# Attention scores of two layers: one fp32 product over padded heads, or three fp32r products over half of TensorE's rows, two heads at a time

## What is computed

```
x = rmsnorm(h);  dq, dk, dv, dg, fq, fk, fv, ff, fg = split(x @ w_in[l])
dq, dk = rope(dq), rope(dk)                      # 4 heads of two halves of 64
do = softmax(q1 k1') v - lam * softmax(q2 k2') v # "diff": mask by chunks of 64
fo = softmax(fq fk' + c_i - c_j) v               # "fox": 8 heads of 64, causal,
                                                 # c = cumsum(log_sigmoid(ff + bias))
h = h + concat(norm(do) * silu(dg), fo * silu(fg)) @ w_out[l]
```

## Time and profile before

| | |
|---|---|
| median of three runs | 1998.08 us |
| the profiled execution | 1999.93 us, of which the span from first to last instruction 1998.1 us |
| mean granted clock of TensorE | 0.989 |
| attention of layer 0, "diff" / "fox" | 228.2 to 287.2 / 287.2 to 362 us |
| attention of layer 1, "diff" / "fox" | 616 to 661.9 / 661.9 to 734 us |

### The profile page before, as it was taken

The page is one execution under the profiler, slowest core; times in us unless marked ns, Lnnn a source line. Parts: engine busy times, 40 slices in busy tenths (PEclk is TensorE's granted clock), DMA queues, the critical chain, the costliest instruction groups (busy, mean ns, idle before and its releaser), DMA issues.

```text
span 1998.1 us, 26646 instructions
## 1 busy us (share of the span) xinstructions
PE 1924.0 (96%) x10942; PEld 1643.1 (82%) x10942; DVE 755.9 (38%) x1288; ACT 707.1 (35%) x1328; POOL 712.7 (36%) x342
## 2 busy tenths in 40 slices
PE   7999989999998999999999999899999989999999
PEld 7999878989987887888888877789767768888887
DVE  6422373454125526441112255546676441111001
ACT  3112355321125545223222223335564542222211
POOL 4333201253332114555554423320003325555443
PEclk9999899999999999999999999899999989999999
DMA  4222200122221002233322233210003212222323
GB/s 142 84 76 84 64 1 1 53 85 85 75 79 48 1 11 89 96 95 95 95 90 93 94 111 117 65 43 1 1 1 112 79 53 94 92 93 93 99 87 108
DMA packets 40585, 144.22 MB, mean 72 GB/s; under 512 B 4624, under 2 KB 4880, under 8 KB 40336
## 3 DMA queue, kind: packets, MB, share of 16 engines
q1 hardware_dynamic: 40464, 142.51, 22.2%
HBM read 140.40 MB, written 2.10 MB: 71 GB/s over the span
## 4 chain that ended last, share of the span: by engine, by line
PE 86%; DVE 7%; ACT 3%; issue 1%; DMA 1%; POOL 1%; SPq 0%; DVEq 0%; ACTq 0%
PE ps L353 22%; PE ps L354 22%; PE ps L355 22%; PE ps L820 5%; PE ps L801 5%; PE ps L810 3%; DMA raw<-wstream 1%; PE ps L1965 1%; PE ps L1948 1%; PE ps L937 1%; PE ps L480 1%; POOL wl L349 1%; ACT wh L341 1%; PE ps L1937 1%; DVE xl L409 1%
## 5 line engine op out<-in xcount | busy, mean ns | idle before, releaser
L349 POOL TENSOR_TENSOR wl<-raw,wh 128x1024 fp32r<-128x1024 f32 (+2 forms) x254 | 604.5, 2380 | 863.7 <-ACT wh L341 863.7
L353 PE MATMUL ps<-xh,wh 128*128 128x512 f32 (+1 forms) x1728 | 622.4, 360 | 26.2 <-POOL wl L349 13.6
L354 PE MATMUL ps<-xl,wh 128*128 128x512 f32 (+1 forms) x1728 | 615.7, 356 | 0.0
L341 ACT ACTIVATE wh<-raw 128x1024 fp32r<-128x1024 f32 (+2 forms) x254 | 266.0, 1047 | 983.9 <-PE ps L355 914.0
L355 PE MATMUL ps<-xh,wl 128*128 128x512 f32 (+1 forms) x1728 | 613.9, 355 | 0.0
L353 PEld LDWEIGHTS ps<-xh,wh 128*128 128x128 f32 x1728 | 327.4, 189 | 82.4 <-issue 20.5
L354 PEld LDWEIGHTS ps<-xl,wh 128*128 128x128 f32 x1728 | 327.7, 190 | 49.8 <-issue 1.9
L355 PEld LDWEIGHTS ps<-xh,wl 128*128 128x128 f32 x1728 | 327.8, 190 | 48.3
L1064 POOL TENSOR_TENSOR xl<-xb,xh 128x512 fp32r<-128x512 f32 (+1 forms) x22 | 26.1, 1185 | 329.2 <-ACT xh L973 329.2
L354 PE MATMUL ps<-aL,wh 128*128 128x512 f32 x352 | 139.3, 396 | 0.0
L355 PE MATMUL ps<-aH,wl 128*128 128x512 f32 x352 | 139.1, 395 | 0.0
(11 more groups left out here) (331 smaller groups left out, 2551.1 us busy)
## 6 DMA issues: line engine op xcount, KB each, us to landing
raw<-wstream SPq DMA_DIRECT2D x236, 512.0 KB, 3.5
raw<-wstream SPq DMA_DIRECT2D x16, 384.0 KB, 3.0
raw<-wstream SPq DMA_DIRECT2D x10, 528.0 KB, 3.5
h<-xT SPq DMA_DIRECT2D x4, 528.0 KB, 6.0
out<-h SPq DMA_DIRECT2D x8, 256.0 KB, 3.4
hm<-memT SPq DMA_DIRECT2D x1, 1024.0 KB, 4.8
cst<-const SPq DMA_DIRECT2D x1, 720.5 KB, 8.9
cst<-const SPq DMA_DIRECT2D x1, 320.0 KB, 4.0
```

Source lines behind the costliest of these rows:

```text
L341: e.activation(wh[p % 2][:, 0:n], raw[c % 2][:, 0:n], ACT.Copy).then_inc(*w_hi(p))
L349: e.tensor_tensor(wl[p % 2][:, 0:n], raw[c % 2][:, 0:n], wh[p % 2][:, 0:n].bitcast(F32), ALU.subtract).then_inc(*w_lo(p))
L353: e.matmul(o, w_h, x_h, start=start, stop=False)
L354: e.matmul(o, w_h, x_l, start=False, stop=False)
```

## The change

Queries and keys of a layer are kept unpadded, two heads to a tile (128 partitions, four tiles), as an fp32r part ("hi") and the rest ("lo"). ACT makes the hi part and POOL the lo part (`whole_hi`, `whole_lo`), two tiles at every second projection tile, behind the weight splits; DVE waits for them (`halved`) before it writes `scratch` or `tmpn` again. The clearing of QA, QB goes. A unit's scores are three fp32r products over the 64 partitions of its head; units m and m + 1, in the two halves of the rows, begin together with their terms interleaved, in different PSUM banks. The forget bias rows stand twice, so that each half of the rows has them. For wide units `begin` comes after the value products (`late`). The meta scores become three products each with 128 columns of weights, even heads first, and odd heads after a wait for the even ones, since all share one bank. Buffers move; `Plan` and `Unit` carry them.

```diff
-                e.tensor_tensor(KA[:, c, :], u, v, ALU.add).then_inc(*roped(*key, "add", 1))
-                for j in range(2):
-                    e.tensor_tensor(QA[64 * j:64 * j + 64, 2 * c + j, c0:c0 + n], ...
+            e.tensor_tensor(u, u, v, ALU.add).then_inc(*roped(*key, "add"))
...
+        def halved(on, key):
+            on.wait_ge(*x_hi[("qk",) + key])
+            on.wait_ge(*x_lo[("qk",) + key])
+        def whole_hi(e, on, key):
+            src, done, dh, _ = whole(key)
+            on.wait_ge(*done)
+            e.activation(dh, src, ACT.Copy).then_inc(*x_hi("qk", *key))
+        def whole_lo(e, on, key):
+            src, _, dh, dl = whole(key)
+            on.wait_ge(*x_hi[("qk",) + key])
+            e.tensor_tensor(dl, src, dh.bitcast(F32), ALU.subtract).then_inc(*x_lo("qk", *key))
...
-            e.tensor_tensor(NCh[32:40, :], ncm, NCh[0:8, :].bitcast(F32), ALU.subtract).then_inc(*v_one("ncl", l))
+            for a in (32, 96):
+                e.tensor_tensor(NCh[a:a + 8, :], ncm, NCh[0:8, :].bitcast(F32), ALU.subtract)
+            e.tensor_copy(NCh[64:72, :], NCh[0:8, :]).then_inc(*v_one("ncl", l))
...
-                for q, Q in enumerate(Q_of[l]):
-                    e.memset(Q[:, :, :], 0.0).then_inc(*p_one("clear", l, q))
-            for q in range(PART["dq", l, 0], PART["gate", l, 7] + 1):
+            p = PART["dq", l, 0]
+            for q in range(p, PART["gate", l, 7] + 1):
                 split_lo(e, on, q + 2)
+                for key in ready_at(q - p, l) if q - p < 15 else ready_at(15, l) if q - p == 16 else ():
+                    whole_lo(e, on, key)
...
+                begun = plan.begin.get(s, [])
+                if begun and units[begun[0]].rows:
+                    a, b = begun
+                    pa, pb = scores(a), scores(b)
+                    for ta, tb in zip(units[a].terms, units[b].terms):
+                        ra = part(pa, units[a], ta)
+                        rb = part(pb, units[b], tb)
+                    ra.then_inc(*score(name, a))
+                    rb.then_inc(*score(name, b))
+                    return
...
-                begin(s)
+                late = any(units[u].banks[1] == 2 for u in plan.begin.get(s, []))
+                if not late:
+                    begin(s)
                 for u in plan.flips.get(s - 1, []):
...
+                if late:
+                    begin(s)
...
-                for m in range(8):
-                    o = ps[0:16, 16 * m:16 * m + 16]
-                    r = e.matmul(o, Q[:, m, 0:16], K[:, m // 2, 0:16], start=True, stop=kind == "diff")
+                for m in (0, 2, 4, 6, 1, 3, 5, 7):
+                    q, o = slice(64 * (m % 2), 64 * (m % 2) + 64), ps[:, 16 * m:16 * m + 16]
+                    if m == 1:
+                        on.wait_ge(*one_mm["meta", kind, l, "even"])
+                    for x, y in ((Qh, Kh), (Qh, Kl), (Ql, Kh)):
+                        r = e.matmul(o, x[q, m // 2, 0:128], y[q, m // 2, 0:16], start=x is Qh and y is Kh, ...
...
-                            terms.append((Q[:, m, c0:c0 + 128], K[:, m // 2, a:b], a, b, True, False))
+                            q = slice(64 * (m % 2), 64 * (m % 2) + 64)
+                            for x, y in ((Qh, Kh), (Qh, Kl), (Ql, Kh)):
+                                terms.append((x[q, m // 2, c0:c0 + 128], y[q, m // 2, a:b], a, b, ...
-                                terms.append((pickR[:, m:m + 1].to_broadcast([128, 128]), NCh[:, a:b], ...
+                                terms.append((pickR[q, m:m + 1].to_broadcast([64, 128]), NCh[q, a:b], ...
...
-                            cols=..., ahead=1 if wide else 2 if beside_meta else 3,
+                            cols=..., ahead=(1 if wide else 2) + m % 2, rows=True, P=..., PT=...,
```

More of the change, by code:

```diff
@@ L182, in program, with flipped @@
         d_x = [sem(f"d_x{i}") for i in range(4)]
+        def flipped(name, at):
+            sb("before" + name, [128, 4, L], at=at)
+            P = sb("Pb" + name, [128, 4, L], at=at)
+            sb("between" + name, [128, 4, L], at=at)
+            return P, [sb(f"PT{name}{i}", [128, 640], at=at) for i in range(2)]
         h = sb("h", [128, KT, L])
         swap = ExitStack()
-        QA1, QB1 = (sb(n, [128, 8, L], at=swap) for n in ("QA1", "QB1"))
+        QhB1, QhA1, QlB1, QlA1 = (sb(n, [128, 4, L], F32R, at=swap) for n in ("QhB1", "QhA1", "QlB1", "QlA1"))
+        swap.close()
+        Pb0, PT0 = flipped("0", swap)
         swap.close()
@@ L294, in program @@
         rT, rTneg, rTm = small[:, 192:200], small[:, 200:208], small[:, 208:210]
-        X, Q_of = {0: (xh, xl), 1: (xh1, xl1)}, {0: (QA, QB), 1: (QA1, QB1)}
+        X = {0: (xh, xl), 1: (xh1, xl1)}
+        QK = {("dq", 0): (QhA, QlA), ("fq", 0): (QhB, QlB), ("dq", 1): (QhA1, QlA1), ("fq", 1): (QhB1, QlB1)}
+        for l in range(2):
+            QK["dk", l], QK["fk", l] = (KhA, KlA), (KhB, KlB)
+        P_of = {(0, "diff"): (Pb0, PT0), (0, "fox"): (Pb1, PT1), (1, "diff"): (Pb1, PT1), (1, "fox"): (Pb0, PT0)}
         freed = [[] for _ in range(8)]
@@ L585, in proj_act @@
                 split_hi(e, on, p + j + 2)
+                for key in ready_at(j, l) if j < 15 else ():
+                    whole_hi(e, on, key)
                 if l == 0 and j == 10:
@@ L595, in proj_act @@
                 split_hi(e, on, PART[v, l, 0] + 2)
+                for key in ready_at(15, l) if v == "va0" else ():
+                    whole_hi(e, on, key)
                 for i in (1, 3):
@@ L778, in slot_read @@
             def slot_read(self, u):
-                was = u - 4 * len(self.sets)
+                was = u - 4 * len(self.units[u].P)
                 if was < 0:
@@ L792, in attention_pe, with scores, part @@
             units, name = plan.units, plan.name
-            def begin(s):
-                for u in plan.begin.get(s, []):
-                    x = units[u]
-                    ps = claim(on, *x.banks, prob[name, u])
-                    for s_, done in x.ready:
-                        on.wait_ge(*s_[done])
-                    for lhsT, rhs, lo, hi, start, stop in x.terms:
-                        r = e.matmul(ps[:, x.o0 + lo:x.o0 + hi], lhsT, rhs, start=start, stop=stop)
+            def scores(u):
+                x = units[u]
+                ps = claim(on, *x.banks, prob[name, u])
+                for s_, done in x.ready:
+                    on.wait_ge(*s_[done])
+                return ps
+            def part(ps, x, term):
+                lhsT, rhs, lo, hi, start, stop = term
+                return e.matmul(ps[:, x.o0 + lo:x.o0 + hi], lhsT, rhs, start=start, stop=stop)
+            def begin(s):
+                begun = plan.begin.get(s, [])
[8 more added lines that the diff above has]
+                    return
+                for u in begun:
+                    x = units[u]
+                    ps = scores(u)
+                    for term in x.terms:
+                        r = part(ps, x, term)
                     r.then_inc(*score(name, u))
@@ L1192, in layer_plan @@
                             last_unit[key] = u
-            return Plan("l%d" % l, units, [Pb1, scratch], PT1, (4, 5), [(tile, ("gate", l, 7))], begins)
+            return Plan("l%d" % l, units, (4, 5), [(tile, ("gate", l, 7))], begins)
         def residual_pe(e, on, name, x, n, c0, put, src=None):
@@ L1916, in nsa_plan @@
                             value=lambda j, rows_, a=a: VSW[:, j, a:a + 64], cols=(64 * m, 64 * m + 64), ahead=2, job=1,
-                            third=3, first=m == 0, last=m == 7, out_bank=NSA_OUT[br]))
+                            third=3, first=m == 0, last=m == 7, out_bank=NSA_OUT[br], P=[Pb2], PT=PT2))
                     last_unit[key] = len(units) - 1
-            return Plan("nsa", units, [Pb2], PT2, (3, 4), [(tile, ("ks", 3))], begins)
+            return Plan("nsa", units, (3, 4), [(tile, ("ks", 3))], begins)
         SB = [(a, j) for a in range(8) for j in (3, 2, 1, 0)]
```

103 lines of the change are left out of this document (53 added, 50 removed).

## The result

The changed kernel takes 2046.98 us (median of four runs, 2039.61 to 2049.47) against 1998.14 (1997.86 to 2000.43): 1.0236 times as long, with a 95% interval of 1.0208 to 1.0264. In the medians that is 48.8 us more, and 23 us above the upper end of the range given. The ratios in this document are of means, without a run that is over 1.5% above the fastest of its kernel. The profiled execution took 2039.61 us, its span is 2037.8; it is the fastest of the four.

What follows compares the result with a forecast made beforehand. PE was taken to bound projections and "fox", a ring of PE and DVE waits "diff". Terms -15.2 + 10.4 + 4.2 + 2.5 = +1.9 us on 1998.08 gave 2000.0 us, range 1988 to 2024.

Steps and rivals of the forecast that it cites:

- The wide "diff" term: Wide "diff" attention: pairs filling all four banks wait for the preceding exponential; loss 5.2 us a layer, bounds 0 and 7.
- the clock, a rival: Wide "diff" attention: PE's clock falls to half, +12.8 us, 2012.8 us in all; chance 0.07.
- Projections: Projection stages: POOL's subtractions, ACT's copies and DVE's new waits fit without delaying PE; cost 0.
- Load and stream: Score products on PE: 128 columns of weights cost at least 0.12 us; streams of 400 columns 0.17, of 512 0.23.
- the switch: Score pairs on PE: the way into half rows and back costs 0.2 us a pair, bounds 0 and 0.2.
- serial loads: Score pairs: loads of the two halves follow each other, two products cost 0.24 us; +22.5 us, 2020.6; chance 0.18.
- loads not hidden: Score pairs: a load doesn't hide behind its own half's stream; +21.5 us, 2019.6; chance 0.04.
- pairs not at once: Score pairs: the two products don't run at once, streams and loads add; +31.3 us, 2029.4; chance 0.08.
- free switching: Score pairs and meta: the way into half rows hides and costs nothing; 9.6 us less, 1990.4; chance 0.22.
- "Fox", a gain of 7.6 a layer: "Fox" scores: paired half-row products take 18.2 us a layer instead of 25.8, if no wait takes PE's place; 15.2 in all.
- Narrow "diff", 0: Narrow "diff" attention: the ring of maximum, exponential and mixing stays and scores come early enough; change 0.
- Meta tokens, 6.7 us: Layer 0's meta scores: short products with 128 weight columns cost 4.2 us more in "fox", 2.5 in "diff"; lower bounds 0.

Runs made afterwards that it cites:

- e14: e10 without the filling products, and meta's "fox" scores begun later, one head a step, the fourth bank kept for them there: 1984.96 us, 0.9931 of the kernel before.
- order-only run: Kernel before with only the changed kernel's order (scores begun in pairs, wide pairs behind the values product), products still fp32 over 128 rows: 2034.6 us, 1.0192.
- e6: Changed kernel with wide "diff" units begun singly, 12 filling products starting each layer's attention, and meta weights of 16 columns instead of 128: 2014.74 us, 1.0092.
- e9: e6 with layer 0's fourth score bank given back to units as soon as meta is through with it: 2007.96 us, 1.0046.
- e13: Changed kernel with meta's "fox" scores moved to the group of 400 keys, the fourth bank kept for them there: 2043.48 us, 1.0238.
- e10: e9 with halves and pairs for the "fox" heads alone, the "diff" heads as in the kernel before: 1998.81 us, 1.0010.
- e2: Changed kernel with its 64-row products, but units begun one at a time, ahead of the values product, with the look-ahead of before: 2104.1 us, 1.0542.
- e7: Changed kernel, wide "diff" singly, 12 filling products per layer, and a full-row fp32 product ahead of layer 0's pairs of 144 or 272 keys: 2026.1 us, 1.0146.

## Why the prediction was wrong

Two steps failed. The wide "diff" term was mis-sized: 5.2 us a layer with 7 as its bound, where 12.4 and 13.4 were lost. And the clock, a rival with 0.07 and in wide "diff" alone, was in the sum at nothing: in the changed kernel's attention TensorE is at half for 126 us instead of 17, first of all behind the meta tokens' scores, which the forecast priced by their own length.

**Projections, at 0: right.** 229.9 against 229.5 us up to the first maximum, 256.1 against 256.2 between the layers. POOL's busy time rose from 712.7 to 738.8 without PE noticing.

**Load and stream right, the switch too cheap**, and the likeliest of the forecasts on how pairs run held. 0.18 us per pair of 400 columns (forecast 0.17), 0.11 at 128. The switch costs 0.09 on the product ahead of the pair, 0.11 on its first and 0.09 on its last, 0.3 us a pair where the forecast had 0.2 as its upper bound, from products over 32 rows. The Trainium skill (TensorEngine Tiling (Array Packing), Tiling Modes) says that tiles in different rows load and multiply in parallel, and the trace agrees: 0.18 us holds two streams of 0.17 and two loads of 0.12. The rivals of serial loads, of loads not hidden and of pairs not at once fall by that row, and free switching by the 0.29 us of the first product.

**"Fox", a gain of 7.6 a layer: mechanism right, somewhat too large.** A wide pair took 1.60 us, as forecast, and one of 272 keys 0.97 (e14, 675.21 to 676.18) where the forecast had 0.92. In e14, whose layer 1 has no fall in its "fox" half, the score products, from the start of each to that of the next, take 18.6 us of PE's time there against 26.4 before: 7.8 saved, as forecast. But from the first "fox" product to the next projection it is 68.5 us against 73.3, a gain of 4.8. Of the other 3.0, 1.6 are in the remaining products, as much as 0.1 ahead of each of 16 pairs comes to, and 1.4 in waits of PE (3.5 against 2.1), the proviso that the forecast had made ("if no wait takes PE's place"). By groups the gain shows at 400 and 528 keys (2.4 and 3.1 us in layer 1). At 144 and 272 together it doesn't (24.5 against 24.6 in e14); the look-ahead has changed, and with it which products of PE fall between two maxima of DVE.

**Wide "diff", a loss of 5.2 a layer with 7 as its bound: mechanism right, mis-sized by more than twice.** In layer 1 it cost 9.0 us in its own group and 3.4 in the one before, 12.4; in layer 0 13.4. The ring was followed from scores over maximum, mixing and exponential back to the banks, 4.72 us, and it came out so: the banks of the second pair are free 4.7 us after its start (692.20 to about 696.9). Measured between pairs were 5.68 (686.52 to 692.20) and 6.48 at the clock's fall; in the order-only run, whose scores are 0.7 longer, 6.35 and 6.21. The first period has the steps that end a block between the maxima, which the forecast had as its bound of 7. The second has what it missed, and what the change's own text shows: wide pairs begin behind the values product, and that product waits for a copy that on DVE stands behind the second maximum. The forecast asked what stands behind a waiting instruction on DVE, and did not ask it for PE. Wide "diff" singly gave 20 us back.

**Narrow "diff", 0: right at full clock, wrong in fact.** With the clock up they are 8.0 and 9.5 us in layer 1 (e6) against 7.3 and 9.6. In the changed kernel layer 1's two groups lost 5.3 and layer 0's two 6.7, to the clock and, in layer 0, to the three banks beside meta, which the forecast did not look at.

**Meta tokens, 6.7 us: the smaller part of their price.** A head's "fox" scores take 0.75 us at full clock (308.66 to 309.41), 6.0 for all; the forecast had 4.8 + 1.6. What was not seen is what follows them: 17 to 31 us at half clock in the profiles of e6 and of e9 to e13 (with a break in e10).

**The clock as a rival: too small and in the wrong place.** It had 0.07 and 12.8 us, in wide "diff". Against it stood that layer 1's "diff" had held 1.00 with PE idle 7 us. That row was of fp32 products over all rows; it said nothing on half rows, as e2 shows, where PE is full and at 0.50 for 64 us. The sign that there was a risk lay in the earlier trace rows: even before, the clock was down right behind layer 0's meta scores (from 233.1, the scores from 232.13, with a wait of PE of 1.5 us ahead of them).

So the forecast of +1.9 became +48.8. In the profiles, over both layers, "fox" at 400 and 528 keys gained 10.9 us of the forecast's 15.2, the wide "diff" pairs cost 25.8 instead of 10.4, and the groups of 144 and 272 keys lost 31.6, where the forecast had 6.7 for meta. The last is for the most part the clock with the waits beside it, 17.1 of it in "fox" of layer 0; how it divides between the two is not measured.

## What to carry to other kernels

When a change queues a long product behind a wait, follow the wait on every engine's queue, PE's own included: what stands behind the waiting instruction there sets the period. A new form of product has to be judged by what it does to TensorE's clock as well as by its slot: read the granted clock and the count of products beside the busy share, and spread runs of short products among long ones. Where a change gives two groups different fates, take it for the group that gains: halves for the "fox" heads alone, with the short scores spread, beat both kernels, by 0.7% and 3%, of which 0.3% against the kernel before is seen in attention itself.

## What the runs showed of the hardware that was not expected

- TensorE's clock fell behind 40 products of 16 columns in a run although PE was busy 7.75 of the 8 us before and 8.00 of 8 behind, and not when the same products were spread over eight steps (29.5 against 20.2 us for the group).
- Once at 0.50 it stayed there for 17 to 31 us in five of the six falls in the changed kernel's attention, beside pairs of half rows, and for 64 us beside single halves, with PE busy 10.00 of 10 us; with the fp32 products over all rows it was at half from 233 to 243 in the kernel before and never for more than 14 us in the order-only run's attention.
- Whether it falls differs between executions of one kernel: e7's four runs span 2015.55 to 2035.75 us, e10's twelve 1993.98 to 2009.77, while e14's six, at a mean clock of 0.988 to 0.991, stay within 1983.22 to 1987.57.
- Twelve products whose result nobody uses gained 5 us in the profile of a layer where they filled the wait ahead of a fall; in two other kernels with them the clock fell there all the same.
- The way from all rows into half rows is paid twice, on the last product ahead (0.20 us instead of 0.11) and on the first pair (0.29 instead of 0.18).
